# Modulation in steps of 32 rows over four groups of partitions, turned once per block, in a two-block network on one core

## The reference, cut to what matters

```
mods = silu(c) @ ada_w[layer] + ada_b[layer]       # [1024] @ [1024, 9216]
h = rms_norm(x, g) * (1 + scale) + shift
x = x + gate * sublayer(h)                          # 0.5 * gate for the FFNs
```

## Time and profile before

| what | value |
|---|---|
| runs | median 1541.31 us (1541.1 to 1542.27, 3 runs) |
| the profiled execution | 1542.63 us, span of its instructions 1540.8 us |
| TensorE busy | 1503.7 us (98%) |
| VectorE, ScalarE busy | 1194.4 us (78%), 888.5 us (58%) |
| mean granted clock of TensorE | 0.990 |
| moved by DMA | 341.72 MB, mean 222 GB/s |

### The profile page before, as it was taken

The page is one execution under the profiler, slowest core; times in us unless marked ns, Lnnn a source line. Parts: engine busy times, 40 slices in busy tenths (PEclk is TensorE's granted clock), DMA queues, the critical chain, the costliest instruction groups (busy, mean ns, idle before and its releaser), DMA issues.

```text
span 1540.8 us, 22921 instructions
## 1 busy us (share of the span) xinstructions
PE 1503.7 (98%) x9384; PEld 1338.2 (87%) x9384; DVE 1194.4 (78%) x1506; ACT 888.5 (58%) x1317; POOL 13.0 (1%) x33
## 2 busy tenths in 40 slices
PE   7999999899999999999999999999999999999998
PEld 6888889698888898888888888888888889988887
DVE  5888879968988769888767698889866566786654
ACT  6665554366655576665567676665755446565542
POOL 2000000000000000000000000000000000000000
PEclk9999999799999999999999999999999999999999
DMA  8988954159989468889453388897665564565552
GB/s 288 319 302 284 315 165 158 36 168 320 335 275 322 156 220 281 292 288 333 146 163 104 116 283 284 278 329 234 217 192 178 177 192 138 164 193 190 185 180 74
DMA packets 295560, 341.72 MB, mean 222 GB/s; under 512 B 6035, under 2 KB 256043, under 8 KB 295456
## 3 DMA queue, kind: packets, MB, share of 16 engines
q1 hardware_dynamic: 293488, 334.72, 65.9%
q0 software_dynamic: 1968, 5.54, 1.0%
HBM read 339.17 MB, written 2.63 MB: 222 GB/s over the span
## 4 chain that ended last, share of the span: by engine, by line
PE 86%; DVE 8%; ACT 5%; issue 1%; DMA 0%; DVEq 0%; ACTq 0%
PE banks L1662 44%; PE banks L1663 22%; PE banks L1594 5%; PE banks L1596 4%; PE banks L1595 4%; DVE arena L1305 2%; ACT w_hi L513 1%; DVE w_lo L982 1%; PE banks L1762 1%; DVE xn L1046 1%; PE banks L1732 1%; ACT xs L539 1%; ACT xn L528 1%; DVE xs L995 1%; PE banks L2028 0%
## 5 line engine op out<-in xcount | busy, mean ns | idle before, releaser
L1662 PE MATMUL banks<-xs,w_hi 128*128 128x512 f32 x1952 | 691.1, 397 | 3.9 <-DVE w_lo L982 3.9
L982 DVE TENSOR_TENSOR w_lo<-raw,w_hi 128x2048 fp32r<-128x2048 f32 (+1 forms) x250 | 558.7, 2238 | 172.6 <-ACT w_hi L513 172.6
L513 ACT ACTIVATE w_hi<-raw 128x2048 fp32r<-128x2048 f32 (+1 forms) x250 | 466.6, 1869 | 194.1 <-PE banks L1663 153.3
L1663 PE MATMUL banks<-xs,w_lo 128*128 128x256 f32 x1952 | 548.5, 281 | 0.0
L1662 PEld LDWEIGHTS banks<-xs,w_hi 128*128 128x128 f32 x1952 | 369.0, 189 | 91.9 <-DVE w_lo L982 5.1
L1663 PEld LDWEIGHTS banks<-xs,w_lo 128*128 128x128 f32 x1952 | 369.5, 189 | 0.0
L1662 PE MATMUL banks<-g_pair,w_hi 128*128 128x512 f32 x1056 | 368.5, 393 | 0.0
L1663 PE MATMUL banks<-g_pair,w_lo 128*128 128x256 f32 x1056 | 295.2, 280 | 0.0
L1662 PEld LDWEIGHTS banks<-g_pair,w_hi 128*128 128x128 f32 x1056 | 198.3, 188 | 43.2
L1090 DVE SCALAR_TENSOR_TENSOR ada_acc<-ada,c_act,ada_acc 128x512 f32<-128x512 f32 x252 | 187.9, 750 | 24.5 <-DMA ada<-in_ada_w 10.8
L1663 PEld LDWEIGHTS banks<-g_pair,w_lo 128*128 128x128 f32 x1056 | 198.3, 188 | 0.0
(11 more groups left out here) (297 smaller groups left out, 1795.6 us busy)
## 6 DMA issues: line engine op xcount, KB each, us to landing
ada<-in_ada_w SPq DMA_DIRECT2D x72, 1024.0 KB, 7.2
raw<-in_ffn_wg SPq DMA_DIRECT2D x44, 1024.0 KB, 5.3
raw<-in_ffn_wu SPq DMA_DIRECT2D x44, 1024.0 KB, 5.4
raw<-in_ffn_w_in SPq DMA_DIRECT2D x43, 1024.0 KB, 5.9
raw<-in_ffn_wd SPq DMA_DIRECT2D x32, 1024.0 KB, 5.3
raw<-in_ffn_w_out SPq DMA_DIRECT2D x16, 1024.0 KB, 5.4
raw<-in_ffn_wd SPq DMA_DIRECT2D x16, 768.0 KB, 4.6
raw<-in_attn_w_qkv SPq DMA_DIRECT2D x12, 1024.0 KB, 5.2
```

The lines of the kernel that those rows point to most:

```text
L513: act.activation(w_hi[:, s, 0:width(c)], raw[:, s, 0:width(c)], ACT.Copy).then_inc(hi_ready, 1)
L982: dve.tensor_tensor(w_lo[:, s, 0:width(c)], raw[:, s, 0:width(c)], w_hi[:, s, 0:width(c)].bitcast(F32), ALU.subtract).then_inc(lo_ready, 1)
L1662: pe.matmul(o, wh[:, k, m], pair, start=first, stop=False, skip_group_check=True)
L1663: return pe.matmul(o[:, 0:T], wl[:, k, m], pair[:, 0, :], start=False, stop=last, skip_group_check=True)
```

## The change

The modulation's matrix is read in another shape. A step now takes 32 rows by all 4608 columns of the half layer, laid over the partitions as four groups: partition `32 q + k` holds row `k`, columns `1152 q` to `1152 q + 1151`. One DMA brings one step (0.59 MB), 32 steps make the half layer, and `ada_flat` serves as a ring of three. VectorE does all of the steps, one per slot in slots 3 to 21, two in six of the later slots, one in slot 32; ScalarE's products and stores go. `silu(c)` is laid out to match on the host (`c_2`), 32 columns of it. The turns move: nine 128 x 128 transposes once per block, on TensorE in stages 1, 6 and 10 ahead of the last square sum, and for the second block behind the plain sums before stage 5. VectorE then adds up each turned tile over 32 columns (`tensor_reduce`, three instructions) and makes the vectors in `norm`, ahead of its wait for `rstd`. The fill matmuls are left out in stages 1, 6 and 10.

```diff
-ADA_W = 512
-ADA_FFN = 9 * D // ADA_W // 2
-ADA_PER = KT - 1
+QUADS = 4
+ADA_W = 9 * D // 2 // QUADS
+ADA_T = D // (P // QUADS)
+ADA_RING = 3
+ADA_TILES = ADA_W // P
...
-ADA_STEPS = {a: 3 if a % 2 else 2 if a in (8, 14, 20) else 1 for a in range(3, GATED)}
-ADA_STEPS.update({23: 4, 24: 3, 26: 4, 27: 3, 29: 4, 30: 3})
+ADA_STEPS = {a: 1 for a in range(3, GATED)}
+ADA_STEPS.update({23: 2, 24: 2, 26: 2, 27: 2, 29: 2, 30: 2, 32: 1})
+ADA_SLOT = [a for a in sorted(ADA_STEPS) for _ in range(ADA_STEPS[a])]
+MOD_AT = {1: 0, 5: 1, 6: 2, 10: 3}
...
+        def ada_slot(i):
+            return ada_flat[:, i % ADA_RING * ADA_W:(i % ADA_RING + 1) * ADA_W]
...
-            def load_ada(f, b, half):
-                done = b + ADA_FFN * f
-                if done:
-                    sp.wait_ge(ada_step, ADA_PER * (done - 1) + (ADA_PER if half else 3))
-                at = (b + f % 2 * ADA_FFN) * ADA_W
-                src = a["ada_w_2"][f // 2, half * 512:(half + 1) * 512, at:at + ADA_W]
-                sp.dma_start(ada[:, half, :].rearrange("p (k n) -> p k n", k=4),
-                             src.rearrange("(k p) n -> p k n", p=P)).then_inc(ada_in[half], 16)
+            def load_ada(f, i):
+                step = ADA_T * f + i
+                if step >= ADA_RING:
+                    sp.wait_ge(ada_step, step - ADA_RING + 1)
+                w = a["ada_w_2"][f // 2, i * P // QUADS:(i + 1) * P // QUADS, f % 2 * QUADS * ADA_W:(f % 2 + 1) * QUADS * ADA_W]
+                sp.dma_start(ada_slot(step), w.rearrange("k (q n) -> q k n", q=QUADS)).then_inc(ada_in[step % ADA_RING], 16)
...
                     if i == 4:
-                        if f:
-                            sp.wait_ge(x_ready, 8 * (n - JOINT[n]))
-                        load_ada(f, 0, 0)
-                        load_ada(f, 0, 1)
+                        if f == 1:
+                            sp.wait_ge(x_ready, 8 * n)
+                        for step in range(ADA_RING):
+                            load_ada(f, step)
+                    for step in range(ADA_RING, ADA_T):
+                        if min(ADA_SLOT[step - ADA_RING] + 5, FFN_CHUNKS - 1) == i:
+                            load_ada(f, step)
...
                     for _ in range(count if f < 4 else 0):
+                        step = ada_at[0]
+                        i = step - ADA_T * f
+                        w, by = ada_slot(step), c_act[:, i:i + 1]
+                        dve.wait_ge(ada_in[step % ADA_RING], 16 * (step // ADA_RING + 1))
+                        if i:
+                            dve.wait_ge(ada_step, step)
+                            ins = dve.scalar_tensor_tensor(out=ada_acc[:, :], in0=w, scalar=by, in1=ada_acc[:, :],
+                                                           op0=ALU.mult, op1=ALU.add)
+                        else:
+                            dve.wait_ge(ev("c_act"), 1)
+                            if f:
+                                dve.wait_ge(ada_summed, f)
+                            ins = dve.tensor_scalar(ada_acc[:, :], w, by, None, ALU.mult)
...
             def modulation(layer, part):
-                dve.wait_ge(ada_stored, ADA_FFN * (2 * layer + part + 1))
+                f = 2 * layer + part
+                dve.wait_ge(ada_summed, f + 1)
+                made = mod[:, layer, 36 * part:36 * part + 36].rearrange("p (q b) -> p b q", q=QUADS)
+                for j, b in enumerate((4, 5, 6)):
+                    n0, n1 = 4 * j, min(4 * j + 4, ADA_TILES)
+                    turned = banks8[:, b, 0:(n1 - n0) * P].rearrange("p (b q k) -> p b q k", b=n1 - n0, q=QUADS)
+                    dve.tensor_reduce(made[:, n0:n1, :], turned, AX_X, ALU.add).then_inc(ada_stored, 1)
+                dve.wait_ge(ada_stored, 3 * (f + 1))
...
+                def turn(f):
+                    pe.wait_ge(ada_step, ADA_T * (f + 1))
+                    for b in range(ADA_TILES):
+                        o = banks8[:, 4 + b // 4, b % 4 * P:(b % 4 + 1) * P]
+                        ins = pe.matmul(o, ada_acc[:, b * P:(b + 1) * P], ident, is_transpose=True, start=(b % 4 == 0),
+                                        stop=True, skip_group_check=True)
+                    ins.then_inc(ada_summed, 1)
...
+                    if k == KT - 1 and n in MOD_AT:
+                        pe.wait_ge(x_ready, 8 * (n - 1) + 6)
+                        turn(MOD_AT[n])
...
+                    if n == 4:
+                        turn(MOD_AT[5])
-                elif n and not after and d is None:
+                elif n and not after and d is None and n not in MOD_AT:
```

More of the change, by code:

```diff
@@ L100, in width @@
     return CH
[L103 to L108 removed]
+ADA_STEPS = {a: 1 for a in range(3, GATED)}
+ADA_STEPS.update({23: 2, 24: 2, 26: 2, 27: 2, 29: 2, 30: 2, 32: 1})
+ADA_SLOT = [a for a in sorted(ADA_STEPS) for _ in range(ADA_STEPS[a])]
+assert len(ADA_SLOT) == ADA_T
+MOD_AT = {1: 0, 5: 1, 6: 2, 10: 3}
 COLS = {}
@@ L143, in two_blocks @@
         ub = sb("ub", [P, KT, T])
-        ada = sb("ada", [P, 2, 4 * ADA_W])
-        ada_acc = [sb(f"ada_acc{i}", [P, ADA_W]) for i in range(2)]
+        ada_flat = sb("ada", [P, 4 * D])
+        ada_acc = sb("ada_acc", [P, ADA_W])
         silu_g = sb("silu_g", [P, 2 * T])
@@ L638, in gu_high @@
                     act.activation(g_pair[:, 0, 2 * s:2 * s + 2, :], two(gu), ACT.Copy).then_inc(guhi_ready, 1)
[L640 to L653, removed]
-                    for j in range(4):
-                        part = turn_bank(b)[:, j * P:(j + 1) * P]
-                        ins = act.activation(part, part, ACT.Copy, accum_out=mod[:, f // 2, at + j:at + j + 1])
-                    ins.then_inc(ada_stored, 1)
[L659 to L663, removed]
-                        if ADA_FROM[b] == a:
-                            ada_product(b)
                 if d:
@@ L1030, in norm @@
                     return
+                if n in MOD_AT:
+                    modulation(MOD_AT[n] // 2, MOD_AT[n] % 2)
                 if n in DEFER:
@@ L1173, in ffn @@
                         split(c0 + a + 2)
+                        ada_part(steps)
                     elif a <= GATED and a % 2 == 0:
@@ L1748, in slot @@
                     return (c0 + a) % SLOTS
-                def turn(b):
-                    done, o = b + ADA_FFN * f, turn_bank(b)
-                    at = ADA_TO[b] + 2
-                    pe.wait_ge(ada_step, ADA_PER * (done + 1))
-                    if done:
-                        pe.wait_ge(ada_stored, done)
-                    if at >= FFN_CHUNKS - len(ROWS):
-                        pe.wait_ge(x_ready, 8 * n + 2)
-                    elif at >= GATED + len(ROWS):
-                        pe.wait_ge(silu_done, s0 + STEPS)
-                    for j in range(4):
-                        ins = pe.matmul(o[:, j * P:(j + 1) * P], ada_acc[done % 2][:, j * P:(j + 1) * P], ident,
-                                        is_transpose=True, start=(j == 0), stop=True, skip_group_check=True)
-                    ins.then_inc(ada_summed, 1)
-                def turned(a):
-                    for b in range(ADA_FFN) if f < 4 else ():
-                        if ADA_TO[b] + 2 == a:
-                            turn(b)
                 if n in DEFER:
@@ L1806, in ffn @@
                     pair, part = divmod(a - GATED, 3)
-                    turned(a)
-                    if pair in (1, 3) and part == 0 and f < 4:
-                        pe.wait_ge(ada_stored, ADA_FFN * f + sum(at + 2 < a for at in ADA_TO))
                     arrived(c0 + a)
```

38 lines of the change are left out of this document (8 added, 30 removed).

## The result

The changed kernel takes 2116.19 us (median, 2103.95 to 2122.36), the kernel before 1541.7 us beside it: a ratio of 1.372, 95% interval 1.369 to 1.374. The profiled execution took 2114.21 us, its span 2112.4 us. The direction and its cause were as forecast, the size was not: +574 us where +380 stood, and 2116 us lies outside the range of 1840 to 2010.

A forecast was written before the change was run, and what follows sets the result against it. TensorE bounds the kernel, DMA close behind; the change makes four DMA engines the bound. From 1541.3 us: +364 loads, +4 skew copy, +8.6 stage beginnings, +3 clock, +380 in sum, about 1922 us; range 1840 to 2010.

The forecast's parts named there:

- Four engines: FFN stages with modulation: new loads, 4 outermost, run on 4 of 16 DMA engines; +364 us in all, chance 0.84.
- Rival A: All 16 engines carry the new loads, split on the destination's 128 partitions; TensorE stays the bound, about 1537.5 us; chance 0.13.
- B's break-even: Eight engines carry the new loads, between hidden and slightly short per slot: +10 to +50 us, 1550 to 1590; chance 0.03.
- the price of a slot: FFN stages with modulation: modulation load 5.85 us plus weight chunk 2.7 gives 8.5 us a slot, against TensorE's 5.6.
- The three slots ahead and three weight slots keep the four engines' queue full: FFN stages with modulation: buffered loads keep the four engines always supplied, so a stage's loads take 263 us without gaps.
- The tail: End of each FFN stage with modulation: some 15 us from the last modulation load until the last column's sum can start.
- Rival C: Four engines, but SP and VectorE waits run their queue dry by 2 us a slot: +250 us more, 2170; chance 0.04.
- The turns: FFN stages: 36 groups of turns removed from TensorE, 0.43 us each, 15.5 us, gained only while TensorE stays the bound.
- Stage beginnings: Stages 1, 5, 6 and 10: turns and VectorE's reductions ahead of the scaling cost 8.6 us, the clock 3 more.
- rival D: The change does little, modulation being hidden anyway: Rival A with the clock's loss whole, within 0.2%; chance 0.05.
- The clock: TensorE's clock may fall inside starved FFN stages, but TensorE has 3 us to spare in each 8.5 there.

The follow-up runs named there:

- loads-alone runs: Changed kernel's loads issued by SP with all computation left out: new load 5.80 us, weight chunk 3.12, both in turn 9.46, chunk with two new loads 16.2 to 16.6.
- rows outermost: Changed kernel with each new load listing its 32 rows first and the four groups second, same bytes and pieces: 1543.28 us, ratio 1.0009 to the kernel before.

## Why the prediction was right, and where it was wrong

**Four engines.** Right, and for the reason given: the copy with eight outermost pointed to it, the trace after shows twos, the new loads alone show a share of 0.25, and the old kernel with this shape loses as much. By the rule that the prediction took from the Trainium skill (DMA: Bandwidth & Descriptors, "Why a DMA increments its semaphore by 16 and not by 1") it is four and eight for these patterns; the trace agrees for both. Rival A's premise (the destination's 128 partitions decide) is false; B's break-even too, as eight engines cost 155 us.

**The steps that failed** are two, both in the sum for a stage. The first is the price of a slot, "One slot then asks 8.5 us of those four engines", and with it the 263 us per stage for 32 loads and 28 chunks. Measured: 310 to 321 us per stage. By the prices of the loads-alone runs a stage asks 19 pairs of 9.46, six tail slots of 16.4, three chunks of 3.12 and one load of 5.8: 293 us. So 30 of the missing 47 to 58 us are prices. A chunk costs 3.1 us and not 2.7, a figure drawn from 3 us of the trace at full rate, which is 12 us for 28 chunks; mixed loads lengthen each other on the mean, some 20 us, half of it in the six slots with two loads to a chunk. The range had the second at up to 15 us a stage and the first at nothing.

The second is "The three slots ahead and three weight slots keep the four engines' queue full". Between the slots it holds, at a stage's beginning it doesn't. The ring holds three loads, and the fourth is issued when VectorE has done the first step, in slot 3: 34 to 43 us after the first load (stage 5: issued at 848.55 and 886.06 us). VectorE's fourth step starts 48.9 to 57.6 us after the first load in the four stages, where four pairs are 37.8 us. These 11 to 20 us are over half of the 17 to 28 us that are left over 293. DMA from 845 to 885 us, at the beginning of stage 5, shows the three loads on four engines (16 twos), then only chunks on all 16, with empty stretches between them (the 1 and the zeros at 870 and 880 us):

```profile
DMA  9910499822222222222222223105998799200399
```

By the packets, 6.4 to 6.6 chunks land in this stretch and not the priced four, as some were on their way before the first load; that is 8 us, an estimate from 3.12 us a chunk, and the rest of the 11 to 20 is not taken apart. Behind the fourth step 5 to 9 us a stage are left: the 15 slots up to the nineteenth step take 9.3 to 9.7 us each, about the 9.46 of the pair, and the tail 117 to 120 us where 113.6 were priced. Over the four stages these misses are what the forecast missed: 2116 against 1922 us, 194. The range's upper end, besides, was drawn at 2010 where its terms give 2014.

**The tail** of 15 us from the last load to the last square sum was right: 344.4 to 360.8 in stage 0, and 14 to 19 us in the others.

**Rival C** had as its sign that stages end later than 278 us after their first load. They did, by 46 to 60 us, and C's 2 us of dry queue in each slot are false all the same: between slots the four engines don't stand idle. A long SP issue (8.29 us above) goes with the queue of those engines being full, the opposite of dry. At the beginning of stage 5 they do run dry, for some 4 us (the row above), once and not in each slot. The sign could not tell a dry queue from slower pieces; the digits of the DMA row can.

**The turns** would have been worth 14.5 us (3.0, 3.5 and 4.0 in stages 0, 2 and 7; stage 5 taken as stage 7), against 15.5, and were not gained, as forecast. **Stage beginnings** cost 13.8 us with rows outermost (3.1, 6.5, 2.0 and 2.2 in stages 1, 5, 6 and 10) against 8.6 plus 3 for the clock: the clock's part is 4.1 in stages 1, 6 and 10, and stage 5's beginning costs 6.5 (its 2.5 in the table and the 4.0 of its turns), clock included, rather than 5. With the loads on 16 engines the change is even, within 0.2%, as rival D had it; A's 1537.5 us was 6 us low, by the beginnings.

**The clock** in the starved stages was granted at 0.81 to 0.83 on the mean; TensorE had time to spare there, as forecast.

## What to carry to other kernels

Before a transfer's bytes are counted, look at the outermost dimension that its pattern has once joinable dimensions are joined: with 4 there, 16 engines become four, and every other load waits behind those four. Price a shared engine by what it takes when both kinds of load run, not by each alone at its best window; where no row shows that, widen the range upwards. Follow the ring of buffers through the first slots of a stage by itself, as a queue that stays full later can run dry there. Spread a short DMA's partitions, and keep TensorE busy through a stage's beginning.

## What the runs showed of the hardware

- Order of dimensions alone: 5.80 us or 1.95 us for the same 0.59 MB in the same pieces of 4,608 B.
- Into 32 adjacent partitions 16 engines, all busy, moved 285 GB/s with a chunk beside, and 360 when the same rows went to every fourth partition.
- SP was held up while the four engines had loads queued: it spent up to 12.6 us on one issue of L372, median 6.0, and 0.5 at the least (duration ns min/median/max):

```profile
L372 SPq DMA_DIRECT2D ada<-in_ada_w x128: 531/5958/12559, 23.1 to 1608.6; - x128
```

- After 3.1 us without work TensorE's clock was granted at 0.50 (1.2 GHz) from 213 to 215 us, and its matmuls of 256 columns, 0.28 us at the start, took 0.41; after 1.4 us without work, with two fill matmuls ahead of it, the clock was 1.00 and they stayed at 0.28.
- With both kinds of load on them DMA was equally busy (share 0.55 and 0.56) at 188 and then at 162 GB/s; the cause is open.
